# Hybrid diffusion step on one core: the second half of the output projection, token tile by token tile, with the norm, transposes and router of other tiles among it

## What is computed

```
merged = jnp.concatenate([rms_norm(attn, ...), rms_norm(sgu, ...), rms_norm(conv, ...)], axis=-1)
x = x + gate1 * (merged @ p['w_out'])
h2 = rms_norm(x, p['norm2']) * (1.0 + scale2) + shift2
x = x + gate2 * hierarchical_moe(h2, router_g_w, router_g_b, router_e_w, router_e_b, moe_w1, moe_w3, moe_w2)
...
# in hierarchical_moe, t = h2 as (tokens, 1024):
g_logits = t @ rg_w + rg_b                      # 4 groups; the best one is taken
e_all = jnp.einsum('td,gde->tge', t, re_w) + re_b   # 4 experts in it; the best two are taken
hid = silu(t @ w1[e]) * (t @ w3[e]);  out += gate * (hid @ w2[e])
```

## Time and profile before

| | us |
|---|---|
| median of 3 runs | 1258.35 |
| the runs | 1258.35, 1257.8, 1263.3 |
| the profiled execution | 1263.37 |
| its span | 1261.4 |
| mean granted TensorE clock in it (share of full speed) | 0.859 |

### The profile page before, as it was taken

One profiled execution on the slowest core, in us unless ns is written; L12 is line 12 of the kernel. 1 busy time (PEld: TensorE's weight loads), 2 busy tenths in 40 slices (PEclk: granted clock), 3 DMA queues, 4 the chain that ended last, 5 costly groups with the idle time before them and its releaser, 6 DMA issues.

```text
span 1261.4 us, 14900 instructions
## 1 busy us (share of the span) xinstructions
PE 1011.3 (80%) x5192; PEld 816.4 (65%) x5192; DVE 725.7 (58%) x952; ACT 609.4 (48%) x904; POOL 280.4 (22%) x312
## 2 busy tenths in 40 slices
PE   3899978997988299998169997999889636999930
PEld 0588866876765078886148886787777535888720
DVE  0367055664434669997446704555533765999826
ACT  1652254654211168897265225544521224988822
POOL 3032052010241112120413305101002502112023
PEclk9999979996995589999569997959789657999965
DMA  9954018271316659998742301716213225999933
GB/s 329 282 213 161 8 46 293 79 256 56 121 67 235 231 211 404 418 413 294 258 165 70 113 30 46 273 54 245 90 34 117 87 96 198 395 411 419 372 134 153
DMA packets 85950, 248.33 MB, mean 197 GB/s; under 512 B 25644, under 2 KB 30252, under 8 KB 75656
## 3 DMA queue, kind: packets, MB, share of 16 engines
q1 hardware_dynamic: 72760, 209.54, 44.8%
q0 software_dynamic: 11696, 32.84, 7.6%
q10 hardware_dynamic: 1440, 5.24, 1.0%
HBM read 221.05 MB, written 30.21 MB: 199 GB/s over the span
## 4 chain that ended last, share of the span: by engine, by line
PE 65%; DVE 11%; DMA 9%; ACT 6%; issue 5%; POOL 4%; SPq 0%; POOLq 0%; ACTq 0%; DVEq 0%
PE ps L1297 11%; PE ps L1299 11%; PE ps L1298 10%; DMA pool<-in_moe_w 4%; PE ps L1304 4%; PE ps L1306 3%; PE ps L1305 3%; PE ps L1432 3%; PE ps L1444 3%; PE ps L1314 3%; PE ps L1446 2%; PE ps L1522 2%; PE ps L1421 2%; PE ps L1550 2%; PE ps L1422 2%
## 5 line engine op out<-in xcount | busy, mean ns | idle before, releaser
L1297 PE MATMUL ps<-wH,actH 128*128 128x512 f32 x608 | 248.5, 409 | 16.2 <-DVE actL L1245 12.0
L1299 PE MATMUL ps<-wH,actL 128*128 128x512 f32 x608 | 241.8, 398 | 0.0
L1298 PE MATMUL ps<-wL,actH 128*128 128x512 f32 x608 | 241.3, 397 | 0.0
L1165 DVE TENSOR_TENSOR wL<-raw,wH 128x2048 fp32r<-128x2048 f32 x64 | 146.0, 2284 | 11.3 <-ACT wH L804 10.6
L1297 PEld LDWEIGHTS ps<-wH,actH 128*128 128x128 f32 x608 | 117.5, 193 | 41.8 <-issue 13.3
L1299 PEld LDWEIGHTS ps<-wH,actL 128*128 128x128 f32 x608 | 116.8, 192 | 26.0
L1298 PEld LDWEIGHTS ps<-wL,actH 128*128 128x128 f32 x608 | 117.4, 193 | 22.9
L804 ACT ACTIVATE wH<-raw 128x2048 fp32r<-128x2048 f32 x64 | 122.0, 1910 | 4.1 <-DMA raw<-in_moe_w 4.1
L1304 PE MATMUL ps<-wH,actH 128*128 128x512 f32 x256 | 105.0, 410 | 4.7 <-DVE wL L1165 3.3
L1306 PE MATMUL ps<-wH,actL 128*128 128x512 f32 x256 | 101.4, 396 | 0.0
L1305 PE MATMUL ps<-wL,actH 128*128 128x512 f32 x256 | 101.1, 395 | 0.0
(11 more groups left out here) (222 smaller groups left out, 1952.5 us busy)
## 6 DMA issues: line engine op xcount, KB each, us to landing
raw<-in_w_ada SPq DMA_DIRECT2D x48, 1024.0 KB, 6.7
raw<-in_moe_w SPq DMA_DIRECT2D x96, 512.0 KB, 7.4
raw<-in_w_in SPq DMA_DIRECT2D x16, 1024.0 KB, 8.4
raw<-in_moe_w SPq DMA_DIRECT2D x16, 1024.0 KB, 11.8
pool<-in_moe_w SPq DMA_DIRECT2D x32, 512.0 KB, 7.4
pool<-in_moe_w SPq DMA_DIRECT2D x16, 1024.0 KB, 10.4
ys<-pool SPq DMA_DIRECT2D x32, 512.0 KB, 10.7
pool<-modrow POOLq DMA_DIRECT2D x16, 512.0 KB, 5.1
```

The source lines that it names most:

```text
L1165: dve.tensor_tensor(wL[:, i, :], mraw[parity][i], f32(wH[:, i, :]), ALU.subtract).then_inc(sem(f"m_lo{i}"), 1)
L1297: pe.matmul(out, aH, wH[:, slot_, cols_], start=first, stop=False)
L1298: pe.matmul(out, aH, wL[:, slot_, cols_], start=False, stop=False)
L1299: return pe.matmul(out, aL, wH[:, slot_, cols_], start=False, stop=last)
```

## The change

The second half of the output projection runs token tile by token tile: for each tile all eight `kt`, with its sums in bank 5 or 7 (`5 + 2 * (t % 2)`). TensorE's queue takes the transposes of tile t-2 and the router of tile t-3 between two tiles. The remaining routers, transposes and `ada_mm` pieces come behind the last tile. GpSimd adds only the first half to `x`; the second half is added by VectorE itself (`second_half`), which then makes `h2b` of the tile before (`normalised`). ScalarE squares the two halves of a row apart, and stores and copies as its queue lists it. GpSimd adds the two sums in its first small instruction. Rows of `h2b`, and so of `h2s` and of the gathered blocks, stay in natural order: `normalised` reads and writes neighbouring places, the router weights are loaded as `(k p)` instead of `(p k)`, and the transposes of a gathered block read every eighth value of a row. Cut to its core:

```diff
 # GpSimd
-for i in range(2 * NT):
-    ... pl.tensor_tensor(xs, xs, otmp[:, i % 4, :], ALU.add).then_inc(sem("x_attn"), 1)
-    ... rstd(stat[:, t:t + 1], stat[:, 8 + t:9 + t], 1, D, sem("ss2"), at("ss2", l, t + 1), sem("rstd2"))
+for t in range(NT):
+    ... pl.tensor_tensor(xs, xs, otmp[:, t % 4, :], ALU.add).then_inc(sem("x_half"), 1)
+for t in range(NT):
+    pl.wait_ge(sem("ss2"), at("ss2", l, NT + t + 1))
+    r = stat[:, 8 + t:9 + t]
+    link(pl.tensor_scalar(r, stat[:, t:t + 1], stat[:, 16 + t:17 + t], EPS, ALU.add, ALU.add))
+    pl.tensor_tensor(r, r, nhalf[:, 0:1], ALU.pow).then_inc(sem("rstd2"), 1)
 # VectorE
+def second_half(t):
+    ... if t == 0: dve.wait_ge(sem("x_half"), at("x_half", l, NT))
+    dve.tensor_tensor(otmp[:, t % 2, :], ps[:, 5 + 2 * (t % 2), :], grow[:, int(t == CTX), N:], ALU.mult)...
+    dve.tensor_tensor(x[:, t, N:], x[:, t, N:], otmp[:, t % 2, :], ALU.add).then_inc(sem("x_attn"), 1)
-    scalar_tensor_tensor(out=hb.rearrange("p (k f) -> p f k", k=KD), in0=by_place(x[:, t, :]), ...)
+    scalar_tensor_tensor(out=hb, in0=x[:, t, :], ...)
 # TensorE
+for t in range(NT):
+    if t >= 2: pe.wait_ge(sem("oproj"), at("oproj", l, NT + t - 1))
+    for kt in range(KD):
+        m = three(ps[:, 5 + 2 * (t % 2), :], ...)
+    if t >= 3: router(t - 3)
+    if t >= 2: h2_chunks(t - 2)
+ada_next(0, 3); router(2); h2_chunks(3); ada_next(3, 5); router(3); h2_chunks(4); ada_next(5, 6); router(4); ada_next(6, KD)
 # transposes of a gathered block
-m = pe.transpose(ps[:, 1 + h, k * P:(k + 1) * P], xg[:, parity, h * N + k * P:h * N + (k + 1) * P], ident[:, :])
+m = pe.transpose(ps[:, 1 + h, k * P:(k + 1) * P], xg[:, parity, :].rearrange("p (f k) -> p k f", k=KD)[:, 4 * h + k, :], ident[:, :])
```

More of the change, by code:

```diff
@@ L788, in _, with mean_square, h2_store, h2T_out @@
                 act.wait_ge(sem("out_done"), 32 * (l + 1))
[L789 to L794, removed]
+                def mean_square(t, half):
+                    act.wait_ge(sem("x_attn" if half else "x_half"), at("x_attn" if half else "x_half", l, t + 1))
+                    if half or t:
+                        act.wait_ge(sem("ss2"), at("ss2", l, NT * half + t))
+                    c = t if half else 16 + t
+                    act.activation(junk2[:, 0:N], x[:, t, half * N:half * N + N], ACT.Square, scale=D ** -0.5,
+                                   accum_out=stat[:, c:c + 1]).then_inc(sem("ss2"), 1)
+                def h2_store(t):
+                    act.wait_ge(sem("h2"), at("h2", l, t + 1))
+                    act.dma_start(h2s[l][t * P:(t + 1) * P, :], h2b[:, t % 2, :]).then_inc(sem(f"h2_stored{t % 2}"), 16)
+                def h2T_out(t):
                     act.wait_ge(sem("h2T_psum"), at("h2T_psum", l, t + 1))
-                    act.dma_start(h2s[l][t * P:(t + 1) * P, :], h2b[:, t % 2, :]).then_inc(sem(f"h2_stored{t % 2}"), 16)
                     if t >= 2:
@@ L801, in _ @@
                                    ACT.Copy).then_inc(sem("h2T"), 1)
+                for t in range(NT):
+                    mean_square(t, 0)
+                mean_square(0, 1)
+                mean_square(1, 1)
+                h2_store(0)
+                mean_square(2, 1)
+                h2_store(1)
+                h2T_out(0)
+                mean_square(3, 1)
+                h2_store(2)
+                h2T_out(1)
+                mean_square(4, 1)
+                h2T_out(2)
+                for t in range(3, NT):
+                    h2_store(t)
+                    h2T_out(t)
                 def m_split(i, parity, pair):
@@ L1114, in _ @@
                     hb = h2b[:, t % 2, :]
[L1116 to L1121, removed]
+                    link(dve.scalar_tensor_tensor(out=hb, in0=x[:, t, :], scalar=stat[:, 8 + t:9 + t], in1=arow[:, c, :],
+                                                  op0=ALU.mult, op1=ALU.mult))
+                    dve.tensor_tensor(hb, hb, srow[:, c, :], ALU.add).then_inc(sem("h2"), 1)
+                dve.wait_ge(sem("a2_row"), at("a2_row", l, 2))
+                dve.wait_ge(sem("shift2_row"), at("shift2_row", l, 32))
+                for t in range(NT):
+                    second_half(t)
+                    if t:
+                        normalised(t - 1)
+                normalised(NT - 1)
+                dve.wait_ge(sem("ss2"), at("ss2", l, 2 * NT))
                 dve.wait_ge(sem("logits"), at("logits", l, NT))
@@ L1477, in _, with ada_next @@
                 merged_chunk(1)
[L1479 to L1504, removed]
+                def ada_next(lo, hi):
+                    if l + 1 < DEPTH:
+                        for n in range(lo, hi):
+                            ada_mm(l + 1, n)
                 def h2_chunks(t):
@@ L1512, in h2_chunks, with router @@
                     m.then_inc(sem("h2T_psum"), 1)
[L1513 to L1519, removed]
+                def router(t):
                     pe.wait_ge(sem("h2T"), at("h2T", l, t + 1))
```

77 lines of the change are left out of this document (55 added, 22 removed).

## The result

The changed kernel takes 1223.57 us (median of 4 runs, 1218.98 to 1226.6), the one before 1260.82 (4 runs, 1257.8 to 1267.8). The ratio is 0.9694, with a 95% interval from 0.9639 to 0.9749: 38.6 us faster, between 31.6 and 45.5. The forecast was 1243, 15 us faster. The time lies in the stated range, which reached to the first rival, but the gain is two and a half times the one forecast: the rival happened. A block's period stayed, 9.38 us against 9.33, which the prediction had named as a sign that it is wrong.

What follows compares the result with a forecast made beforehand. TensorE was taken as the bound, through its waits and lower clock. Logits 35.4 us earlier over both layers, less 20.2 for stepped loads, gave 15.2 off the median of 1258.35: 1243 us, range 1232 to 1251.

Steps and rivals of the forecast that it cites:

- the first rival: Expert loop's transposes: TensorE reads with a step at no cost; 1223 us, down to 1213 at full clock; chance 0.28.
- A block's period: Expert loop, transpose to transpose: 9.33 us before, near 9.95 forecast; staying at 9.33 would show the prediction wrong.
- The projection runs through: Output projection's second half: TensorE runs on without waiting for VectorE tile by tile, last tile ending at 371.0.
- Bank 5 for tile 2: Projection's second half: TensorE wants the bank at 350.9, VectorE has read it at 350.5; it just fits.
- The logits of layer 0: Behind layer 0's projection: logits at 393.2 against 411.0, 17.8 us won, or 22.8 at full clock.
- what is left is what ran at 0.59 before: Layer 0's last routers, transposes and piece: lower clock assumed, 3.5 us a router, 1.9 for transposes or a piece.
- The wait for piece 4: Layer 0, among the last routers: piece 4 lands at 381.3, a new TensorE wait of 0.9 us.
- The logits of layer 1: Behind layer 1's projection, without pieces: logits at 1002.1 against 1019.7, 17.6 us won; router 2 at 1.9 us.
- The expert loop: Transposes of gathered blocks: stepped weight loads cost 0.105 us each, 192 showing, 20.2 us lost, 26.9 if all show.
- the other three have nothing to hide them: Each group of four block transposes: only the first load lies under a matmul, so 6 of 8 a block show.
- a slower kernel: Block transposes: stepped load costs more than the logits win, a transpose going from 0.11 to 0.36 us; 1287 us; chance 0.09.
- the DMAs as the bound: Expert loop: DMA bounds it, so a longer TensorE block hides behind the loads; 1223 us; chance 0.08.

Runs made afterwards that it cites:

- e7: Changed kernel with layer 0's modulation pieces 0 to 3 one behind each last tile's transposes and the last router, 4 to 7 behind the counting matmuls: 1219.03 us.
- e5: Changed kernel with all eight of layer 0's modulation pieces moved from among the routers to behind the counting matmuls: 1231.02 us, single run.
- e6: Changed kernel with four thrown-away matmuls in each of layer 1's three waits for ScalarE's copy: 1222.06 us, ratio 0.9712.
- e1: Changed kernel with rows of h2 reordered again as before the change, block transposes reading neighbouring values: 1232.76 us, ratio 0.9757.

## Why the prediction was wrong, point by point

- **The projection runs through: right.** The wait for bank 0 went. Bank 5 for tile 2 was named as a close fit, and TensorE took it without a pause; the transposes of tile 0 found h2b ready at 355.67 + 1.23 = 356.9 (rows below), 0.2 us ahead of TensorE at 357.09, where 0.4 was worked out. The last tile's end was put at 371.0; this execution's mark lies 0.75 us later, so 371.75, and the trace has 371.52.

```profile
354.35 1.28 DVE L1148 SCALAR_TENSOR_TENSOR pool<-x,stat,pool 128x1024 f32<-128x1024 f32 x1 [0.86 <-POOL stat L554]
355.67 1.23 DVE L1150 TENSOR_TENSOR pool<-pool 128x1024 f32<-128x1024 f32 x1
```

- **The logits of layer 0: mechanism right, clock wrong.** The forecast took the lower clock from piece 4 on and got 17.8 us; it gave 22.8 for the full clock, and 22.3 came. The step that failed is "what is left is what ran at 0.59 before". First, 0.59 is a mean that did not stand for what is left: routers 3 and 4 took 4.05 us for both in the kernel before (rows below), where half speed is 3.60 for one. Second, in the kernel before a piece stood in front of every router but the last too, and transposes, pieces and routers ran on at half speed behind a wait of 2.70 us for h2b, although TensorE was busy for 19.00 of 19.00 us. In the changed kernel TensorE comes to them from the projection with the clock up, and with pieces in the waits it stays up: e7 has the order of before, transposes, one piece, router, with routers of 1.96 us. e5 leaves the waits empty, and the clock falls. That the clock at which TensorE arrives makes this difference is read from these rows; no run changed it by itself. The wait for piece 4 was 0.41 us and not 0.9; pieces 5 to 7 waited too, which I had not worked out.

```profile
388.73 1.97 PE L1511 MATMUL ps<-ident,pool 128*128 128x128 f32 x8 [2.70 <-DVE pool L1120]
390.62 1.94 PE L1314 MATMUL ps<-raw,cpad 128*32 128x512 f32 x8
...
406.85 4.05 PE L1522 MATMUL ps<-rw,pool 128*128 128x20 f32 x32
```

- **The logits of layer 1: nearly right.** 16.8 against 17.6 us: the clock fell in router 2 already, which I had put at 1.9 us and which took 2.99.
- **Behind the logits, layer 0: a term was missing.** The last pieces stand ahead of the counting matmuls on TensorE's queue. Before, they were done in time; now their DMAs, requested one after the other, were late: 1.2 us lost.
- **The expert loop: the step that failed.** "The nearest row is VectorE's", 0.105 us more for each of 192 transposes, 20.2 us. It is 0.05 us a block, 1.6 us in all. VectorE's rate for a stepped input does not carry over to TensorE's weight load, which gets longer by about 50 ns while one load still starts 0.11 us after the other. The step broke at "the other three have nothing to hide them": they overlap one another. The evidence lay in the trace of the kernel before and I did not use it: four transposes in 0.44 us, with loads that are recorded longer (139 ns, shown above) than the 110 ns from one transpose to the next, so that loads must already overlap. A delay added to overlapped loads is not a rate. The rule of the Trainium skill that was weighed there ("Advanced Engine Details and Errata", section SBUF Cachelines) agrees with VectorE's second norm instruction, which took 2.02 us where it read one input with the step and takes 1.23 without. On TensorE it shows in the recorded length of a load, 190 ns against 139, and not in the time from one transpose to the next.
- **The sum.** 15.2 forecast, plus 18.6 (step), plus 4.5 (clock, layer 0), less 0.8 (layer 1), less 1.5 (logits to first block) is 36.0 us; measured 38.6, between 31.6 and 45.5. The first rival, at 1223, is what happened, with 0.28 where 0.55 went to the forecast. Its mechanism, no cost of the step, is what the runs show; that its time was met within 1 us is partly luck, since it had layer 0's clock 4.5 us wrong as well, and two other terms went the other way. The two rivals of a slower kernel and of the DMAs as the bound fell: transposes are as long as before, and so is the period.

## What to carry to other kernels

When instructions of an engine overlap, a longer one can cost next to nothing: here 50 ns more a load cost 2 to 3 ns a transpose in a long row, and 6 in the loop (0.05 us for the eight of a block). How much longer a load can get before it shows was not tried. Before pricing a slower load, compare its recorded length with the distance from one to the next. A reordering that one engine does at 1 us an instruction may be free as an access pattern of another; try it where a transpose reads the data anyway. And where short matmuls wait a microsecond for another engine, put useful matmuls into the wait (here of 512 columns), or even some that are thrown away: it was worth 6 us a layer here, by the stages (47.8 to 41.9 us in layer 0 from e5 to e7, in layer 1 from the changed kernel to e6).

## What the runs showed of the hardware

Work that is thrown away makes a stage shorter: 12 small matmuls that compute nothing take 5.9 us off it (47.8 to 41.9). With the three waits of 1.11 us left empty, TensorE's clock was 0.50 among routers and transposes; with them filled it was 1.00. The order of the instructions alone does not decide it: transposes, one piece and a router ran at half speed in the kernel before, behind a wait for h2b, and at full speed in e7, behind the projection.

The other surprise is where the spread of the times comes from. The same instructions of the attention stretch run at different granted clocks in different executions. The stretch in layer 0 in the changed kernel's first profile, in the same kernel profiled again (a2) and in e1, and in layer 1 of the kernel before (columns as above):

```profile
215.00:250.00 35.00, 31.10 (x222) 27.66 (x222) 21.62 (x37) 19.65 (x43) 5.73 (x13) 0.90 0.24 75
```

```profile
215.00:250.00 35.00, 31.95 (x173) 30.50 (x172) 18.71 (x31) 17.16 (x37) 5.14 (x11) 0.66 0.19 63
```

```profile
215.00:250.00 35.00, 31.69 (x154) 30.09 (x153) 16.96 (x28) 15.34 (x34) 5.62 (x12) 0.60 0.22 75
```

```profile
820.00:855.00 35.00, 32.14 (x145) 30.58 (x145) 18.10 (x30) 15.23 (x34) 2.78 (x6) 0.56 0.14 48
```

At 0.60 TensorE gets through 154 instructions in the 35 us instead of 222, and the mark behind it comes at 353.1 instead of 343.6. a2 is the changed kernel itself: its mark comes at 349.8, and its "between" takes 347.4 us instead of 340.8. This is up to 10 us a layer that has nothing to do with any edit here; of the 41.1 us between the two profiled spans 6.8 are of this kind. Why the clock falls in one execution and not in another was not tried.
